# Retention with both directions stacked on 128 partitions, and another order of the attention steps, in a two-block transformer kernel

## The chip, the cores and the metric

The kernel runs on one core of one Trainium2 chip. The metric is the device time of one execution in microseconds (us); smaller is better. The engines are called as the profile calls them: PE (TensorE, the matrix engine), DVE (VectorE), ACT (ScalarE), POOL (GpSimd) and SP (the queue that issues most transfers). Each runs its own program in order; they meet at semaphores.

## What is computed

Two transformer blocks on one sequence of 512 tokens with 1024 features, all in float32. The first block (feed-forward, gated linear attention with convolution, feed-forward) is not touched. In the second, one projection feeds a neighbourhood attention (8 heads, 4 column blocks) and a bidirectional retention (4 heads, 4 chunks of 128 tokens). The part that the change rewrites, cut from the reference:

```python
def retention_scan(q, k, v, log_gamma, include_diag):
    ...
    s = jnp.einsum('bnihd,bnjhd->bnhij', qc, kc) * dmat
    intra = jnp.einsum('bnhij,bnjhe->bnihe', s, vc)
    zeta = jnp.exp(log_gamma[:, None] * (c - 1 - idx)[None, :])
    chunk_kv = jnp.einsum('bnjhd,hj,bnjhe->nbhde', kc, zeta, vc)
    ...
    _, prev = lax.scan(step, jnp.zeros((bsz, heads, dk, dv), F32), chunk_kv)
    xi = jnp.exp(log_gamma[:, None] * (idx + 1.0)[None, :])
    cross = jnp.einsum('bnihd,nbhde,hi->bnihe', qc, prev, xi)
    return (intra + cross).reshape(bsz, seq, heads, dv)

def bidirectional_retention(q, k, v, lg_fwd, lg_bwd):
    flip = lambda t: jnp.flip(t, axis=1)
    fwd = retention_scan(q, k, v, lg_fwd, True)
    bwd = flip(retention_scan(flip(q), flip(k), flip(v), lg_bwd, False))
    return fwd + bwd
```

A head has 64 query and key features and 128 value features. The sum over both directions is normalised per head (`head_group_norm`), gated by a SiLU and stands beside the attention's output before the product with `w_out_2`.

## The kernel before

**Units.** The whole program is a list of units. A unit is the product of one weight block of 1024 x 128 with the activations: 8 slices of 128 rows, each with three products of 128x512 (high part by high, low by high, high by low: lines 1294 to 1296), so 24 products. Unit u needs its weights split: a transfer brings them to `raw`, ACT copies them to `wh` (`hi`, line 360), DVE subtracts to get `wl` (`lo`, line 714). Three buffers go round, so at unit u ACT and DVE prepare unit u+2, and ACT may only do so once unit u-1 is done.

**The stage.** The change lies in the 16 units from `U0["rot"]`: I call them steps 0 to 15. Steps 0 to 3 make the rotary queries and keys (`RQ`, `RK`), steps 4 to 11 the attention's queries and keys (`NQ`, `NK`), steps 12 to 15 the gates. Retention and attention are cut into pieces that are written between the units by hand, in one loop `for n in range(16)` in each engine's program. On PE a piece stands in the middle of the unit (`ret_mid`, after 12 of its 24 products) or behind it. Nothing but this written order decides what runs when.

**Attention.** A piece p (0 to 15) is a pair of heads hp = p // 4 and a column block p % 4. Pieces go in pairs: `na_s(p)` on PE makes the scores of p and p+1 (line 1582, banks 3 and 4); DVE adds the bias and takes the maxima (`na_s`, lines 1127 and 1129), ACT takes the exponentials (`na_e`, line 611), DVE divides by the sums (`na_x`, lines 1136 to 1139), PE transposes (`na_t(p)`, line 1594, bank 5 for even p and 3 for odd p), ACT copies the transposed scores out (`na_t`, line 616), PE multiplies with the values (`na_o(p)`, line 1606, bank 6). POOL prepares the bias tiles (line 341).

**Retention.** Two heads share the 128 partitions of `RQ` and `RK`. PE transposes the keys of a pair (`ret_k`, line 1516), ACT scales them into `KF` and `KB` (line 590), PE makes the chunk states forward and backward (`ret_kv`, line 1529, 64 columns of a head at a time), DVE runs the recurrences (lines 1096 and 1099) into `SF` and `SB` and scales the queries (`ret_q`, lines 1106 and 1108) into `QF` and `QB`. Per head: `ret_s(h)` makes the scores (line 1540), DVE applies the decay (line 1113), `ret_o(h)` makes the output in bank 2 from 10 products (line 1552 within the chunk, lines 1554 and 1556 across chunks, these on the head's 64 partitions), ACT copies and squares it (lines 602 and 603), `ret_n(h)` sums the squares over the partitions in bank 7 (line 1324), DVE makes the mean (line 730), ACT the inverse root (`rows`, lines 370 to 374), DVE corrects it and scales the output (`ret_y`, lines 734, 736 and 1119). Before the change step n of the loop has, behind the unit on PE, `na_t(p)`, `na_t(p + 1)`, `na_o(p)`, `na_o(p + 1)` with p = 2(n - 7), and `na_s(p + 2)`.

Of the kernel before, what the change touches and what calls it, by code (L numbers as in the profile page):

```python
# [1852 lines left out]
```

## Time and profile before

| what | us |
|---|---|
| median of 3 runs | 1859.44 (1859.05 to 1859.75) |
| the profiled execution, its own time | 1860.06 |
| span from its first to its last instruction | 1858.3 |
| PE busy | 1833.1 |
| DVE busy | 968.1 |
| ACT busy | 618.3 |

The rows in the section further down are of these kinds. The page sums busy time by engine and follows back the chain of work that ended last. A row of the timeline has the start in us from the span's start, how long the merged instructions took, engine, line, operation, tiles written and read, shapes and count; in brackets the engine's idle time ahead of it and what ended it. Products overlap in the pipeline, so the distance between two starts says what a product costs, and not its own duration. A float32 product of the small pieces shows as two records. A row of the windows view gives for one stretch the busy time of each engine with the number of its instructions, and behind them the granted clock of PE as a share of full speed (1.00 is 2.4 GHz, 0.50 is 1.2 GHz).

### The profile page before, as it was taken

What the parts mean: (1) busy time and instruction counts of PE and PEld (TensorE: products, weight loads), DVE (VectorE), ACT (ScalarE), POOL (GpSimd) and SP (SyncE); (2) the same over time, 40 slices, a digit from 0 to 9 for tenths busy, and PEclk for the clock granted to TensorE, in tenths of its full rate; (3) what the DMA queues carried; (4) which work ended last, traced back from release to release, by engine and by line L of the source; (5) the groups of instructions that cost most, each with busy time, mean ns of one, the idle gap of its engine ahead of it and who ended that gap; (6) DMA issues with size and microseconds to landing.
All of it is one profiled execution on the core that took longest, in us unless ns stands there. A gap on an engine that the chain in (4) does not pass through costs nothing.

```text
span 1858.3 us, 20334 instructions
## 1 busy us (share of the span) xinstructions
PE 1833.1 (99%) x8370; PEld 1507.5 (81%) x8370; DVE 968.1 (52%) x1275; ACT 618.3 (33%) x881; POOL 33.5 (2%) x34
## 2 busy tenths in 40 slices
PE   8999999999999999999999999999999999999998
PEld 6888888878888888888888888888776788888887
DVE  6444434637765534455543443465567664535354
ACT  6222313344332223323422222244445432222133
POOL 0000000000000000000000000000221000000000
PEclk9999999999999999999999999999999999999999
DMA  5332332332122232323233233233411233232322
GB/s 172 93 101 94 99 102 85 97 103 80 57 91 95 98 102 91 102 91 102 91 102 96 98 92 101 87 98 128 131 41 46 82 100 102 92 102 91 102 91 69
DMA packets 52812, 176.38 MB, mean 95 GB/s; under 512 B 6336, under 2 KB 9024, under 8 KB 52720
## 3 DMA queue, kind: packets, MB, share of 16 engines
q1 hardware_dynamic: 51520, 172.51, 29.0%
q8 instruction: 67, 1.10, 0.2%
q0 software_dynamic: 448, 1.24, 0.2%
q10 hardware_dynamic: 752, 1.33, 0.2%
q14 instruction: 25, 0.20, 0.0%
HBM read 170.86 MB, written 2.10 MB: 93 GB/s over the span
## 4 chain that ended last, share of the span: by engine, by line
PE 94%; DVE 3%; ACT 2%; issue 1%; DMA 0%; SPq 0%; DVEq 0%
PE ps L1294 28%; PE ps L1295 28%; PE ps L1296 28%; PE ps L1314 2%; PE ps L1316 1%; PE ps L1315 1%; DVE wl L714 1%; PE ps L1324 0%; PE ps L1450 0%; PE ps L1582 0%; PE ps L1552 0%; DVE tm L1127 0%; PE ps L1453 0%; PE ps L1438 0%; DVE X L800 0%
## 5 line engine op out<-in xcount | busy, mean ns | idle before, releaser
L1294 PE MATMUL ps<-Hhi,wh 128*128 128x512 f32 x1544 | 610.9, 396 | 6.8 <-DVE Hlo L719 6.8
L1295 PE MATMUL ps<-Hlo,wh 128*128 128x512 f32 x1544 | 603.0, 391 | 0.0
L1296 PE MATMUL ps<-Hhi,wl 128*128 128x512 f32 x1544 | 602.9, 390 | 0.0
L714 DVE TENSOR_TENSOR wl<-raw,wh 128x1024 fp32r<-128x1024 f32 (+1 forms) x320 | 388.0, 1213 | 127.1 <-ACT wh L360 125.0
L360 ACT ACTIVATE wh<-raw 128x1024 fp32r<-128x1024 f32 (+1 forms) x320 | 332.3, 1039 | 321.3 <-PE ps L1296 301.4
L1294 PEld LDWEIGHTS ps<-Hhi,wh 128*128 128x128 f32 x1544 | 291.0, 188 | 73.8 <-issue 11.1
L1295 PEld LDWEIGHTS ps<-Hlo,wh 128*128 128x128 f32 x1544 | 291.2, 189 | 61.9 <-issue 2.6
L1296 PEld LDWEIGHTS ps<-Hhi,wl 128*128 128x128 f32 x1544 | 291.0, 188 | 61.2
L1294 PE MATMUL ps<-Ahi,wh 128*128 128x512 f32 x792 | 308.2, 389 | 0.3 <-DVE Alo L1155 0.3
L1296 PE MATMUL ps<-Ahi,wl 128*128 128x512 f32 x792 | 308.1, 389 | 0.0
L1295 PE MATMUL ps<-Alo,wh 128*128 128x512 f32 x792 | 308.1, 389 | 0.0
L762 DVE TENSOR_TENSOR tm<-ps,R 128x512 f32<-128x512 f32 x128 | 88.5, 691 | 197.5 <-PE ps L1296 197.4
L1294 PEld LDWEIGHTS ps<-Ahi,wh 128*128 128x128 f32 x792 | 148.7, 188 | 31.5 <-DVE Alo L1155 0.7
L1296 PEld LDWEIGHTS ps<-Ahi,wl 128*128 128x128 f32 x792 | 148.7, 188 | 30.9
L1295 PEld LDWEIGHTS ps<-Alo,wh 128*128 128x128 f32 x792 | 148.7, 188 | 30.8
L770 DVE TENSOR_TENSOR Alo<-tm,Ahi 128x512 fp32r<-128x512 f32 x92 | 63.7, 692 | 70.5 <-ACT Ahi L402 34.2
L800 DVE SCALAR_TENSOR_TENSOR X<-ps,X 128x512 f32<-128x512 f32 x48 | 33.1, 690 | 96.7 <-PE ps L1296 96.7
L766 DVE TENSOR_TENSOR X<-ps,X 128x512 f32<-128x512 f32 x47 | 32.5, 691 | 95.5 <-PE ps L1296 95.5
L402 ACT ACTIVATE Ahi<-tm 128x512 fp32r<-128x512 f32 x44 | 27.8, 633 | 163.2 <-DVE tm L792 163.2
L387 ACT ACTIVATE tm<-tm 128x512 f32<-128x512 f32 x44 | 27.8, 632 | 163.1 <-DVE tm L762 163.1
L792 DVE TENSOR_TENSOR tm<-ps,tm 128x512 f32<-128x512 f32 x44 | 30.4, 691 | 77.1 <-PE ps L1296 77.0
L676 ACT ACTIVATE Ahi<-tm 128x512 fp32r<-128x512 f32 x32 | 20.2, 633 | 124.1 <-DVE tm L1224 124.1
(256 smaller groups left out, 1192.2 us busy)
## 6 DMA issues: line engine op xcount, KB each, us to landing
raw<-in_w_gu SPq DMA_DIRECT2D x87, 512.0 KB, 3.3
raw<-in_w_d SPq DMA_DIRECT2D x32, 512.0 KB, 3.5
raw<-in_w_up SPq DMA_DIRECT2D x32, 512.0 KB, 3.3
raw<-in_w_dn SPq DMA_DIRECT2D x32, 512.0 KB, 3.6
raw<-in_w_d SPq DMA_DIRECT2D x16, 384.0 KB, 3.1
raw<-in_w_v SPq DMA_DIRECT2D x8, 512.0 KB, 3.6
raw<-in_w_cc SPq DMA_DIRECT2D x8, 512.0 KB, 3.3
raw<-in_w_cu SPq DMA_DIRECT2D x8, 512.0 KB, 3.4
```

Source lines behind the costliest of these rows:

```text
L360: act.activation(WH[u % 3][:, 0:n], RAW[u % 3][:, 0:n], ACT.Copy).then_inc(s["wh"], 1)
L387: act.activation(TA[2 + j % 2], TA[j % 2], ACT.Silu).then_inc(s["silu"], 1)
L714: dve.tensor_tensor(WL[u % 3][:, 0:n], RAW[u % 3][:, 0:n], f32(WH[u % 3][:, 0:n]), ALU.subtract).then_inc(s["wl"], 1)
L762: dve.tensor_tensor(dst, BK[BANK[u]][:, :], R[:, :], ALU.mult).then_inc(s["ev"], 1)
L766: dve.tensor_tensor(X[:, n, :], BK[BANK[u]][:, :], X[:, n, :], ALU.add).then_inc(s["ev"], 1)
L770: dve.tensor_tensor(Alo[:, j, :], src, f32(Ahi[:, j, :]), ALU.subtract).then_inc(s["al"], 1)
L792: dve.tensor_tensor(TA[6 + j % 2], BK[BANK[u + 1]][:, :], TA[4 + j % 2], ALU.mult).then_inc(s["ev"], 1)
L800: dve.scalar_tensor_tensor(out=X[:, n, :], in0=BK[BANK[u]][:, :], scalar=0.5, in1=X[:, n, :], op0=ALU.mult, op1=ALU.add).then_inc(s["ev"], 1)
L1294: pe.matmul(ps, wh[:, c], hi[:, k, :], start=(k == 0), stop=False)
L1295: pe.matmul(ps, wh[:, c], lo[:, k, :], start=False, stop=False)
L1296: last = pe.matmul(ps, wl[:, c], hi[:, k, :], start=False, stop=(k == nb - 1))
L1314: pe.matmul(ps, Hhi[:, k, tc], wh[:, c], start=(k == 0), stop=False)
```

## The change

**Both directions on one set of partitions.** For each head, forward keys stand in columns 0 to 63 and backward keys in columns 64 to 127 of `KFB`; a product `ret_kv(h)` gives both states of a chunk in 128 partitions, four per head. The states lie in `SFB[h]` (forward in partitions 0 to 63, backward in 64 to 127, zeros where a direction has no earlier chunk) and the scaled queries likewise in `QFB[h]`, each with a buffer of its own per head. `ret_o(h)` is then 8 products over all 128 partitions instead of 10. ACT copies the first state of each direction (`ret_kv` on ACT), DVE sets zeros and does the rest. The scores of two heads are made together (`ret_s(hp)`), in two banks (`RB_S`). Outputs and states take banks from `RB_O` and `RB_KV`, and `ret_n(h)` writes its sums over the bank of the output that has been copied out.

**Another order.** The pieces of retention stand at other places (listed below the diff). On PE the outputs of the attention come one step later, between the two transposes, which both use bank 5: `na_t(p)`, `na_o(p - 2)`, `na_o(p - 1)`, `na_t(p + 1)`, `na_s(p + 2)` in every step; a third buffer (`PT`) holds the copies. On DVE `lo(u + 2)` now stands ahead of `na_x(p)`, and `ret_kv`, `ret_mean` and `ret_y` behind it. On ACT `rows` and `ret_o` stand ahead of the copies of the transposed scores in steps 9 to 11 (`rows` alone in 11). `na_s(12)` and `na_s(14)` move from the middle of units 12 and 13 to behind units 12 and 13. The transfers of `VB` are issued three units earlier on SP.

```diff
@@ tiles
-    RT_S, RT_Q, RT_G, RT_O = [1, 0, 2, 1], [2, 1, 0, 2], [0, 1, 0, 2], [2, 1, 0, 1]
+    RT_S, RT_Q, RT_G = [1, 0, 0, 2], [2, 1, 1, 0], [2, 1, 0, 2]
+    RB_S, RB_O, RB_KV = [5, 4, 2, 6], [2, 7, 2, 7], [2, 6, 5, 6]
+    PT = [TA[4], TA[5], PT2[:, :]]
@@ ACT
+        def ret_kv(h):
+            kv = four(BK[RB_KV[h]][:, :])
+            act.wait_ge(s["rkv"], h + 1)
+            act.activation(SFB[h][0:64, 1, :], kv[0:64, 0, :], ACT.Copy).then_inc(s["rkc"], 1)
+            act.activation(SFB[h][64:P, 2, :], kv[64:P, 3, :], ACT.Copy).then_inc(s["rkc"], 1)
...
-            act.activation(TA[4 + p % 2], BK[3 if p % 2 else 5][:, :], ACT.Copy).then_inc(s["ntc"], 1)
+            act.activation(PT[p % 3], BK[5][:, :], ACT.Copy).then_inc(s["ntc"], 1)
...
+            if n == 6:
+                ret_o(0)
+                ret_o(1)
+                ret_kv(2)
+                ret_kv(3)
+            if n in (7, 9, 10, 11):
+                rows(7 + (7, 9, 10, 11).index(n), TA[6], TA[7], TA[8])
+            if n in (9, 10):
+                ret_o(n - 7)
             if 7 <= n < 15:
                 na_t(p)
+                if n in (9, 11, 13):
+                    na_o((n - 9) // 2)
                 na_t(p + 1)
...
-            if 6 <= n < 12:
+            if 6 <= n < 14:
                 na_e(p + 2)
...
-            if n in (6, 7, 9, 10):
-                rows(7 + (6, 7, 9, 10).index(n), TA[6], TA[7], TA[8])
@@ DVE
+        def ret_kv(h):
+            kv = four(BK[RB_KV[h]][:, :])
+            own.add(dve.memset(SFB[h][0:64, 0, :], 0.0))
+            own.add(dve.memset(SFB[h][64:P, 3, :], 0.0))
+            dve.wait_ge(s["rkc"], 2 * h + 2)
+            for step in range(2):
+                own.add(dve.scalar_tensor_tensor(out=SFB[h][0:64, 2 + step, :], in0=SFB[h][0:64, 1 + step, :],
...
+            lo(u + 2)
             if 7 <= n < 15:
                 na_x(p)
-            lo(u + 2)
...
+            if n == 5:
+                ret_kv(0)
+                ret_kv(1)
+                ret_s(0)
+                ret_s(1)
+                ret_q(2)
...
+            if n == 7:
+                ret_kv(2)
+                ret_kv(3)
+                ret_mean(0)
+            if n == 8:
+                ret_s(2)
                 ret_s(3)
...
+            if 9 <= n < 13:
+                ret_y(n - 9)
+                if n < 12:
+                    ret_mean(n - 8)
@@ PE
+        def ret_o(h):
+            b = RB_O[h]
+            pe.wait_ge(s["rst"], h + 1)
+            pe.wait_ge(s["rq"], h + 1)
+            pe.wait_ge(s["rsd"], h + 1)
...
+                pe.matmul(BK[b][:, tc], RV[:, c, h * P:h * P + P], RT[RT_S[h]][:, tc], start=True, stop=False)
+                p = pe.matmul(BK[b][:, tc], SFB[h][:, c, :], QFB[h][:, tc], start=False, stop=True)
...
         def na_t(p):
-            b = 3 if p % 2 else 5
             pe.wait_ge(s["nxd"], p + 1)
-            if p >= 2:
-                pe.wait_ge(s["ntc"], p - 1)
...
+            if p == 0:
+                pe.wait_ge(s["rst"], 3)
+            else:
+                pe.wait_ge(s["ntc"], p)
...
             if n == 4:
-                ret_k(0)
+                ret_s(0)
             if n == 5:
-                ret_s(0)
+                ret_o(0)
             if n == 6:
-                na_s(0)
-                ret_n(0)
+                ret_kv(1)
             if 7 <= n < 15:
                 na_t(p)
+                if n == 7:
+                    ret_s(1)
+                else:
+                    na_o(p - 2)
+                    na_o(p - 1)
                 na_t(p + 1)
...
+            if 6 <= n < 14:
                 na_s(p + 2)
```

In the middle of the units PE now has `ret_k(0)` in step 3, `ret_kv(0)` (heads 0 and 1) in 4, `ret_k(1)` in 5, `ret_o(1)` and `ret_n(0)` in 6, `ret_n(1)` in 7, `ret_o(2)` in 9, `ret_n(2)` and `ret_o(3)` in 10, `ret_n(3)` in 11 and `na_o(14)`, `na_o(15)` in 15.

**Where it shows: ACT in step 9.** Line 360 (362 after the change) is the copy `hi` of the weights, 602 and 603 (611 and 612) copy and square a retention output, 616 (625) copies transposed scores, 611 (620) is an exponential, 370 to 374 (372 to 376) are `rows`. Before:

```order
L360 ACTIVATE wh1_58<-raw1_55 128x1024 [waits s_pe,s_raw1]
L602 ACTIVATE YH_123<-ps 128x512 [waits s_ro]
L603 ACTIVATE SS_64<-ps 128x512
L616 ACTIVATE tm4_70<-ps 128x512 [waits s_nat]
L616 ACTIVATE tm5_71<-ps 128x512 [waits s_nat]
L611 ACTIVATE tm2_68,small_82<-tm2_68,small_82 128x256 [waits s_nmx]
```

and after:

```order
L362 ACTIVATE wh1_58<-raw1_55 128x1024 [waits s_pe,s_raw1]
L372 ACTIVATE tm7_73<-tm6_72 128x512 [waits s_nm]
L374 ACTIVATE tm7_73<-tm7_73 128x512 [waits s_ao]
L376 ACTIVATE tm8_74<-tm7_73 128x512 [waits s_ao]
L611 ACTIVATE YH_127<-ps 128x512 [waits s_ro]
L612 ACTIVATE SS2_65<-ps 128x512
L625 ACTIVATE tm5_71<-ps 128x512 [waits s_nat]
L629 ACTIVATE Ahi_52<-ps 128x512 [waits s_nop]
L625 ACTIVATE PT2_124<-ps 128x512 [waits s_nat]
```

The three instructions of `rows`, the first of which waits for DVE's mean (`nm`), have moved from behind the step's exponentials to ahead of its first copy of transposed scores.

**DVE in step 9.** Line 714 (731) is `lo`; 1136 to 1139 (1165 to 1168) are `na_x`; 734, 736 and 1119 (751, 753 and 1148) are `ret_y`; 1113 is a decay of scores, 730 (1143) the mean. Before:

```order
L1136 RECIPROCAL small_82<-small_82 128x2 [waits s_nex]
L1138 TENSOR_SCALAR tm1_67<-tm1_67,small_82 128x256 [waits s_vo]
L1139 TENSOR_SCALAR tm1_67<-tm1_67,small_82 128x256
L714 TENSOR_TENSOR wl1_61<-raw1_55,wh1_58 128x1024 [waits s_wh]
L1113 TENSOR_TENSOR SS2_65<-ps,DG_113 128x512 [waits s_rsc]
L1187 SCALAR_TENSOR_TENSOR NK_102<-ps,R_63 128x512 [waits s_pe]
```

and after:

```order
L731 TENSOR_TENSOR wl1_61<-raw1_55,wh1_58 128x1024 [waits s_wh]
L1165 RECIPROCAL small_82<-small_82 128x2 [waits s_nex]
L1167 TENSOR_SCALAR tm0_66<-tm0_66,small_82 128x256 [waits s_vo]
L1168 TENSOR_SCALAR tm0_66<-tm0_66,small_82 128x256
L1165 RECIPROCAL small_82<-small_82 128x2 [waits s_nex]
L1167 TENSOR_SCALAR tm1_67<-tm1_67,small_82 128x256 [waits s_vo]
L1168 TENSOR_SCALAR tm1_67<-tm1_67,small_82 128x256
L751 SCALAR_TENSOR_TENSOR tm6_72<-tm8_74,tm6_72 128x512 [waits s_na]
L753 SCALAR_TENSOR_TENSOR tm6_72<-tm6_72,tm7_73 128x512 [waits s_vo]
L1148 TENSOR_TENSOR YH_127<-YH_127,tm6_72 128x512 [waits s_vo]
L1143 TENSOR_SCALAR tm6_72<-ps 128x512 [waits s_vo,s_nsum]
```

The weights' `lo` now stands ahead of `na_x`, and the mean for which ACT's `rows` waits is the last of the eleven.

**PE behind unit 9.** Line 1594 (1620) transposes, 1606 (1634) is the attention's output, 1582 (1609) its scores. Before:

```order
L1594 MATMUL ps<-ident_77,tm0_66 128x128 [waits s_ntc,s_nxd]
L1594 MATMUL ps<-ident_77,tm0_66 128x128 x3
L1594 MATMUL ps<-ident_77,tm1_67 128x128 [waits s_ntc,s_nxd]
L1594 MATMUL ps<-ident_77,tm1_67 128x128 x3
L1606 MATMUL ps<-tm4_70,VB_103 64x128 [waits s_nal,s_ntc]
```

and after:

```order
L1620 MATMUL ps<-ident_77,tm0_66 128x128 [waits s_ntc,s_nxd]
L1620 MATMUL ps<-ident_77,tm0_66 128x128 x3
L1634 MATMUL ps<-PT2_124,VB_103 64x128 [waits s_vb2,s_ntc]
L1634 MATMUL ps<-PT2_124,VB_103 64x128 x3
L1634 MATMUL ps<-tm4_70,VB_103 64x128 [waits s_vb3,s_ntc]
L1634 MATMUL ps<-tm4_70,VB_103 64x128 x3
L1620 MATMUL ps<-ident_77,tm1_67 128x128 [waits s_ntc,s_nxd]
L1620 MATMUL ps<-ident_77,tm1_67 128x128 x3
L1609 MATMUL ps<-NK_102,NQ_101 128x256 [waits s_nsd,s_ev]
```

The outputs of the step before stand between the two transposes, and the second transposes wait for the copy of the first (`ntc`).

## Rows read from the trace of the kernel before

**Rows 1.** The page: busy time of PE; the chain that ended last, by engine.
```profile
PE 1833.1 (99%) x8370; PEld 1507.5 (81%) x8370; DVE 968.1 (52%) x1275; ACT 618.3 (33%) x881; POOL 33.5 (2%) x34
...
PE 94%; DVE 3%; ACT 2%; issue 1%; DMA 0%; SPq 0%; DVEq 0%
```

**Rows 2.** Windows (us): busy by engine, PEclk, DMA; the stage, and a stretch behind a wait.
```profile
1300.10:1453.05 152.95, 143.91 (x817) 111.59 (x816) 98.20 (x168) 75.85 (x165) 29.96 (x24) 0.99 0.23 70
...
1338.90:1342.40 3.50, 3.50 (x10) 2.68 (x10) 1.43 (x2) 0.00 (x0) 0.00 (x0) 0.51 0.41 118
```

**Rows 3.** Timeline of PE: units, retention's pieces, two waits.
```profile
1300.10 0.39 PE L1294 MATMUL ps<-Hhi,wh 128*128 128x512 f32 x1
...
1327.08 0.39 PE L1296 MATMUL ps<-Hhi,wl 128*128 128x512 f32 x1
...
1330.61 0.88 PE L1529 MATMUL ps<-RV,KF 128*64 128x128 f32 x12
...
1332.07 0.50 PE L1294 MATMUL ps<-Hhi,wh 128*128 128x512 f32 x1
...
1337.32 1.16 PE L1540 MATMUL ps<-RQ,RK 64*128 64x128 f32 x8 [2.19 <-DVE QB L1108]
...
1342.85 0.39 PE L1552 MATMUL ps<-SS,RV 128*128 128x128 f32 x2
...
1347.20 0.53 PE L1294 MATMUL ps<-Hhi,wh 128*128 128x512 f32 x1
...
1351.28 1.12 PE L1324 MATMUL ps<-RS,ones 128*128 128x512 f32 x2
...
1355.00 0.38 PE L1552 MATMUL ps<-SS,RV 128*128 128x128 f32 x2
...
1358.67 0.50 PE L1294 MATMUL ps<-Hhi,wh 128*128 128x512 f32 x1
...
1427.38 0.63 PE L1594 MATMUL ps<-ident,tm 128*128 128x128 f32 x4 [1.50 <-DVE tm L1127]
```

**Rows 4.** Timeline of PE in the first block: 28 small records on all 128 rows.
```profile
475.56 0.60 PE L1450 MATMUL ps<-ST,VT 128*128 128x128 f32 x4
...
478.69 0.49 PE L1419 MATMUL ps<-ident,KS 128*128 128x128 f32 x3
```

**Rows 5.** Timeline of PE behind unit 10: transposes, scores, outputs, sum of squares.
```profile
1403.57 1.04 PE L1594 MATMUL ps<-ident,tm 128*128 128x128 f32 x8
1405.43 1.14 PE L1582 MATMUL ps<-NK,NQ 64*128 64x256 f32 x8 [0.83 <-ACT tm L616]
1406.50 1.15 PE L1606 MATMUL ps<-tm,VB 128*64 128x128 f32 x16
1407.58 1.13 PE L1324 MATMUL ps<-RS,ones 128*128 128x512 f32 x2
```

**Rows 6.** Timeline of DVE around steps 6 and 7, and one recurrence.
```profile
1332.87 0.73 DVE L1099 SCALAR_TENSOR_TENSOR SF<-SF,small,ps 128x128 f32<-128x128 f32 x2
...
1351.41 0.69 DVE L1127 TENSOR_TENSOR tm<-ps,tm 128x512 f32<-128x512 f32 x1 [0.40 <-PE ps L1582]
...
1354.05 0.68 DVE L730 TENSOR_SCALAR tm<-ps 128x512 f32<-128x512 f32 x1
1354.65 0.16 DVE L1136 RECIPROCAL small<-small 128x2 f32<-128x2 f32 x1
...
1355.11 0.35 DVE L1139 TENSOR_SCALAR tm<-tm,small 128x256 f32<-128x256 f32 x1
...
1358.09 1.22 DVE L714 TENSOR_TENSOR wl<-raw,wh 128x1024 fp32r<-128x1024 f32 x1 [1.90 <-ACT wh L360]
1359.23 0.69 DVE L734 SCALAR_TENSOR_TENSOR tm<-tm,tm 128x512 f32<-128x512 f32 x1
...
1360.68 0.69 DVE L1119 TENSOR_TENSOR YH<-YH,tm 128x512 f32<-128x512 f32 x1
```

**Rows 7.** Timeline of ACT: steps 6 and 7, and the start of the gates.
```profile
1355.17 0.61 ACT L370 ACTIVATE tm<-tm 128x512 f32<-128x512 f32 x1
...
1357.02 1.04 ACT L360 ACTIVATE wh<-raw 128x1024 fp32r<-128x1024 f32 x1
1358.78 0.60 ACT L602 ACTIVATE YH<-ps 128x512 f32<-128x512 f32 x1 [0.72 <-PE ps L1554]
...
1439.87 1.28 ACT L625 ACT_TABLE_LOAD   x1
...
1443.15 1.04 ACT L360 ACTIVATE wh<-raw 128x1024 fp32r<-128x1024 f32 x1
```

More of the change, by code:

```diff
@@ L566, in act_program @@
         act.wait_ge(s["lgv"], 2)
-        own.add(act.activation(E128, LG[:, 8:12], ACT.Exp, scale=128.0))
+        own.add(act.activation(E128, LG[:, 12:16], ACT.Exp, scale=128.0))
         act.wait_ge(s["dgm"], 1)
@@ new lines, in ret_q @@
+        def ret_q(h):
+            hs = slice(64 * (h % 2), 64 * (h % 2) + 64)
+            dve.wait_ge(s["rot"], 1 + h // 2 * 2)
+            dve.wait_ge(s["rxf"], h // 2 * 2 + 2)
+            own.add(dve.tensor_tensor(four(QFB[h][0:64, :]), four(RQ[hs, h // 2, :]),
+                                      XF[hs, :].unsqueeze(1).broadcast_to([64, 4, P]), ALU.mult))
+            dve.tensor_tensor(four(QFB[h][64:P, :]), four(RQ[hs, h // 2, :]),
+                              XB[hs, :].unsqueeze(1).broadcast_to([64, 4, P]), ALU.mult).then_inc(s["rq"], 1)
@@ L1116, in ret_y, with ret_mean @@
+        def ret_s(h):
+            dve.wait_ge(s["rsc"], h // 2 + 1)
+            dve.tensor_tensor(four(RT[RT_S[h]]), four(BK[RB_S[h]][:, :]),
+                              DG[:, h, :].unsqueeze(1).broadcast_to([P, 4, P]), ALU.mult).then_inc(s["rsd"], 1)
+        def ret_mean(h):
+            dve.wait_ge(s["nsum"], 7 + h)
+            own.wait()
+            dve.tensor_scalar(TA[6], BK[RB_O[h]][:, :], 1.0 / P, EPS, ALU.mult, ALU.add).then_inc(s["nm"], 1)
         def ret_y(h):
@@ L1533, in ret_s @@
-        def ret_s(h):
-            hs = slice(64 * (h % 2), 64 * (h % 2) + 64)
-            if h % 2 == 0:
-                pe.wait_ge(s["rq"], h // 2 + 1)
-            else:
-                pe.wait_ge(s["rsd"], h)
+                pe.wait_ge(s["rsd"], 1)
+                pe.wait_ge(s["rst"], 2)
+            for h in (2 * hp, 2 * hp + 1):
+                for c in range(4):
+                    p = pe.matmul(BK[RB_KV[h]][:, c * P:c * P + P], KFB[:, h % 2, c, :], RV[:, c, h * P:h * P + P],
+                                  start=True, stop=True)
+                p.then_inc(s["rkv"], 1)
@@ L1539, in ret_s @@
+        def ret_s(hp):
+            pe.wait_ge(s["rot"], 2 * hp + 2)
+            if hp == 1:
+                pe.wait_ge(s["nm"], 7)
+                pe.wait_ge(s["rst"], 4)
             for c in range(4):
[L1540 to L1541 removed]
+                for j in range(2):
+                    hs, b = slice(64 * j, 64 * j + 64), RB_S[2 * hp + j]
+                    p = pe.matmul(BK[b][:, c * P:c * P + P], RK[hs, hp, c * P:c * P + P], RQ[hs, hp, c * P:c * P + P],
+                                  start=True, stop=True)
```

224 lines of the change are left out of this document (89 added, 135 removed).

## The prediction, made before the changed kernel was run

> **What bounds the kernel now.** I read the page first: PE is busy 99% of the span and makes up 94% of the chain that ended last [rows 1]. So a change pays what it takes from PE or makes PE wait, and nothing else. The windows view then bounds the stage: steps 0 to 15 last 152.95 us [rows 2]. All that the change moves lies there (the earlier `VB` transfers reach back a little, onto a queue that runs three units ahead). In the timeline, 120 products of five units run from 1300.10 to the start of the last at 1327.08 [rows 3]: 26.98 / 119 = 0.227 us each, 5.44 us a unit, 87.0 us for 16 units. The other 66 us are small pieces, waits, and one stretch at half the clock. The longest wait is 2.19 us, for DVE's `QB` [rows 3]; behind it PE ran at a granted clock of 0.51 for 3.5 us [rows 2], in which 10 records stand where 3.5 / 0.227 = 15 would elsewhere. At 1.2 GHz for 3.5 us half of it is lost: 1.8 us.
>
> **The small pieces, priced.** On all 128 rows of the array, 28 float32 records take 478.69 - 475.56 = 3.13 us, 0.112 each [rows 4].
> - `ret_o`, before: 1355.00 to the next unit product at 1358.67 is 3.67 us a head [rows 3]. After: 8 products, 16 records, all on 128 rows as in rows 4: 16 x 0.112 = 1.79. Four heads: -7.5 us.
> - `ret_kv`, before: 1330.61 to 1332.07 is 1.46 us a pair [rows 3], 24 records at 0.061, two halves of 64 columns side by side. After: 16 records on the whole array, 1.79. Two pairs: +0.7. Here a rule speaks against the change. The Trainium skill (TensorEngine Tiling (Array Packing), Theoretical Speedup) gives up to twice the speed for products at most 64 wide on a tiled array. The trace agrees (0.061 against 0.112); stacking gives this up, and by the rule or by the rows the loss is the same small one.
> - Retention's scores, before: about 1.1 us where they stand alone (8 records, 1.16 with their tail) and 0.7 at the end of `ret_o` (1342.85 to 1347.20 is 4.35, less 3.67) [rows 3], some 3.4 for four heads. After, two heads on two row groups. Attention's scores are built like that: 8 records of 256 columns in 1406.50 - 1405.43 = 1.07 us [rows 5], 0.13 each, though 256 columns one after the other would need 0.22. So a pair costs between 1.1 (overlapped) and 1.8 (not); I take 1.1: -1.2.
> - Unchanged in work: four transposes 0.45, attention scores 1.07, a pair of outputs 1.08 (1406.50 to 1407.58), a sum of squares 0.9 of the 1.13 it shows [rows 5]. One more change of array shape per step (transposes, outputs, transposes, scores): 0 to 0.2 each, within the rounding of the steps below.
>
> If nothing ever waited, the steps would add up to 129 us, 131 with the shape changes: 22 us below the stage of before. So the question is who is late.
>
> **The chain behind the scores.** In steps 7 to 14 PE needs the normalised scores of the pair that it made at the end of the step before. I call the end of those scores E; it is the start of the next unit. From rows, with E of step 6 at 1351.28, where the sum of squares takes over on PE [rows 3] (DVE starts at 1351.41 [rows 6]):
> - bias, maxima, exponentials: ACT's next work starts at 1355.17 [rows 7], E + 3.9.
> - `hi`, next in ACT's order: 1.04 [rows 7]. `lo` follows 1.07 behind `hi`'s start (1357.02, 1358.09): starts at E + 4.95. The next DVE work starts 1.14 later (1359.23) [rows 6]: E + 6.1.
> - the first half of `na_x`: 1354.65 to 1355.11 + 0.35 = 0.81 [rows 6]: E + 6.9; both halves 1.54: E + 7.65.
>
> Before, `na_x` stood ahead of `lo`: its first half was done at 1355.46, E + 4.2, sooner than the unit. Now PE is ready for the transposes at E + 5.45 in a step with nothing in mid unit, and waits 1.5 us. The order rows of DVE leave no other way.
>
> In steps 9 to 11 it goes on. DVE does `ret_y`, 1359.23 to 1360.68 + 0.69 = 2.14 [rows 6], then the mean (0.68, as at 1354.05): E + 10.45. ACT's `rows` wait for that mean: 1355.17 to 1357.02 = 1.85: E + 12.35. In steps 9 and 10 ACT then copies and squares a retention output, about 0.5 apiece since 0.60 overlaps the next [rows 7]: E + 13.3. Only then comes the copy of the first transposed scores, of the same form and so 0.6: E + 13.9. PE's second transposes need that copy, since both write bank 5. They start at E + 14.0 in steps 9 and 10, at E + 13.0 in 11. Queued behind them on PE are the next scores, and behind these the next unit and the next chain: nothing can run ahead.
>
> **The steps after, one by one (us).** 0 to 2: 16.3. 3: unit, four transposes, and 0.3 of waiting for the rotated keys (DVE ends `turn(1)` about when mid unit comes; 0 to 0.3): 6.2. 4: unit + 1.79 + 1.1 = 8.3. 5: unit + 0.45 + 1.79, and a wait of 1.0 (DVE: `turn(3)`, `lo`, two recurrences, a decay; a recurrence is 2 x 0.65 by the 0.73 of a pair of steps [rows 6], plus 0.25 for the zeros, ahead of which POOL's bias tiles may slow `lo`; 0.7 to 1.3): 8.7. 6: unit + 1.79 + 0.9 + 1.79 + 1.07 = 11.0. 7: `na_t(0)` waits for `ret_kv(2)` as well, since bank 5 held those states: 7.65 + 1.55 = E + 9.2 instead of 6.35; retention's scores wait for the other recurrence and the mean, E + 11.4; then 1.1 + 0.45 + 1.07: 14.1. 8: transposes at 7.0, outputs wait for two decays on DVE (7.65 + 1.3 = 8.95), then 1.08 + 0.45 + 1.07: 11.6. 9 and 10: 14.0 + 0.45 + 1.07 = 15.6 each. 11: 14.6. 12 and 13: 7.0 + 0.45 + 1.08 + 0.45 + 1.07 = 10.2 each (with the shape changes). 14: ACT has taken up the gate's table load and first gate ahead of `hi`. From the load at 1439.87 to `hi` at 1443.15 is 3.3 [rows 7], so `hi` ends at 3.9 + 3.3 + 1.04 = 8.3, `lo` at 9.5, the first half of `na_x` at E + 10.3; then 0.45 + 1.08 + 0.45: 12.4. 15: unit + 1.1 + 0.2 = 6.7. Behind it nothing is late that was not before.
>
> Sum: 161.5, against 152.95: **+8.5 us**. It contains 32 us of PE waiting, where before PE was idle for 152.95 - 143.91 = 9 [rows 2] and the slow clock cost 1.8.
>
> **The clock.** The trace has one fall to 1.2 GHz in the stage, behind a wait of 2.19 us; behind the wait of 1.50 at 1427.38 [rows 3] it stayed at 2.4. The new waits of steps 7 (3 and 1.7), 9 (5), 10 (4), 11 (4.5) and 14 (4.8) are all as long or longer, so I expect a fall at each, worth up to 1.8 by the row. Where a unit runs slowly and the next step waits anyway, the loss is absorbed; only the transposes and scores ahead of the next E count, about 1 us each in steps 7 to 11, and all 1.8 in 14: +6, with 0 and +10 as ends. The Trainium skill (TensorE: Matmul & The Clock Gate, What's actually happening) says that the gate's resting state is the slow one and that activity releases it; by that rule each long wait costs, which agrees with the one fall seen. It gives no other sum.
>
> **Forecast.** +8.5 + 6 = +14.5 us on the profiled execution's own 1860.06 (its span 1858.3 and 1.8 around it): 1874.6. That execution is 0.6 above the median, so the median comes to **1874.0**.
>
> **Rivals.**
> - *The clock does not fall, or only where it is absorbed.* For it: only one fall in 153 us so far. Time 1859.4 + 8.5 = 1868. Chance 0.15.
> - *The clock stays low over steps 7 to 11.* Against it: the fall seen lasted 3.5 us with PE busy. It decides once the small pieces between waits are too little activity to bring it back: each step's tail of 2.7 us then takes up to twice as long and units of 10 us exceed the first transposes' time by 3: +24 in all, 1883. Chance 0.08.
> - *Faster.* DVE and ACT keep up after all and the change keeps its shorter PE work: mechanism and place would be `ret_y` and the mean of steps 9 to 11 done while DVE waits for `wh` rather than behind it. In-order engines forbid this by the order rows; it would need E + 14.0 to shrink below PE's own 8.9 to 9.8. Up to -22: 1838. From a shortening of the chains of steps 9 to 11 by 3 us each on, the sign turns if the clock also holds. Chance 0.08.
> - *Chains shorter than priced by 1 to 2 us each,* as when DVE overlaps more than rows show: 1862 to 1867, of which half lies within 0.2%. Chance 0.07.
>
> The forecast's own case has the remaining 0.62, between 1868 and 1880. The range 1863 to 1883 leaves out the faster rival and a bit on each side, under 2 in 10. About 0.2% (3.7 us) is what a measurement of this kernel can tell from no change. Slower by more: 0.62 + 0.15 + 0.08 + 0.03 = 0.88; within: 0.04; faster: 0.08.
>
> **What would show it.** Right: a wait of some 5 us ahead of the second transposes of step 9, put down to ACT's copy, 4 or more in 10 and 11; about 1.5 us ahead of the first transposes of steps 12 and 13, put down to `na_x`; 2.8 us ahead of `na_t(0)` with the recurrence as releaser; some 4.8 in step 14. Outputs of retention 1.8 us a head. Several stretches at a granted clock of 0.5. Wrong: second transposes of step 9 before E + 10, steps 9 and 10 shorter than 12 us each, or PE's small records of `ret_o` farther apart than 0.112.

## The result, and the profile after

The changed kernel takes **1880.1 us** in the median (1879.1 to 1880.9, four runs), the kernel before 1859.45 (1859.05 to 1859.75) beside it. The ratio is 1.011, with a 95% interval of 1.009 to 1.013: the change makes the kernel about 20 us slower. The forecast was 1874.0 with a range of 1863 to 1883. The profiled execution of after took 1880.53 us, 0.4 above its median, so its trace can be read as it stands.

The page of after, against [rows 1]: PE busy, the chain that ended last by engine, and the granted clock in 40 slices.

```profile
PE 1835.7 (98%) x8338; PEld 1510.0 (80%) x8338; DVE 970.2 (52%) x1291; ACT 621.5 (33%) x889; POOL 31.8 (2%) x34
...
PEclk9999999999999999999999999999988999999999
...
PE 92%; DVE 4%; ACT 2%; issue 1%; DMA 0%; SPq 0%; DVEq 0%
```

PE has 32 matmul records fewer than before (8338 against 8370) and is busy 2.6 us *longer*; two slices of the clock are down. The windows view of after says where: the stage (steps 0 to 15), and two stretches in which the clock was down. Columns as in [rows 2]: length, busy time by engine, granted clock, DMA.

```profile
1300.02:1473.31 173.29, 146.27 (x785) 114.12 (x784) 100.25 (x184) 79.12 (x173) 28.29 (x24) 0.90 0.20 63
...
1361.95:1372.19 10.24, 7.75 (x34) 5.86 (x35) 4.87 (x9) 4.17 (x9) 2.51 (x2) 0.50 0.01 2
...
1392.67:1399.50 6.83, 4.22 (x15) 2.90 (x16) 1.74 (x3) 3.51 (x7) 2.51 (x2) 0.50 0.01 2
```

The stage went from 152.95 us [rows 2] to 173.29, +20.3, which is the whole difference of the spans (1878.5 - 1858.3 = 20.2). PE is not busy for 173.29 - 146.27 = 27.0 us of it, where it was 9.0 before. And the clock of TensorE is at half (1.2 GHz) in five stretches of 10.2, 6.8, 3.4, 6.8 and 6.8 us, 34 us in all, where before there was one of 3.4.

Who is waited for, by the waits view of PE in the stage of after (total us, times, longest):

```profile
PE ps L1620 <- ACT tm L625: 9.2, 3, 5.0
PE ps L1620 <- DVE tm L1168: 5.8, 2, 4.6
PE ps L1620 <- ACT PT L625: 4.2, 1, 4.2
PE ps L1620 <- DVE SFB L1117: 3.0, 1, 3.0
PE ps L1574 <- DVE tm L1143: 2.1, 1, 2.1
PE ps L1634 <- DVE RS L1137: 1.4, 1, 1.4
PE ps L1589 <- DVE SS L1137: 1.3, 1, 1.3
```

L1620 are the transposes of the attention weights, L625 ACT's copy of transposed weights out of PSUM, L1168 the normalisation `na_x`. Before, the transposes waited twice for DVE, 1.5 us [rows 3] and 0.5, and never for ACT's copy.

The longest wait, in step 9, is followed here through the timelines of DVE, ACT and PE, put together in order of time. The step starts at E = 1381.20, with the unit behind the scores.

```profile
1386.15 1.22 DVE L731 TENSOR_TENSOR wl<-raw,wh 128x1024 fp32r<-128x1024 f32 x1 [2.11 <-ACT wh L362]
1387.30 0.16 DVE L1165 RECIPROCAL small<-small 128x2 f32<-128x2 f32 x1
...
1388.75 0.69 DVE L751 SCALAR_TENSOR_TENSOR tm<-tm,tm 128x512 f32<-128x512 f32 x1
...
1390.99 0.69 DVE L1143 TENSOR_SCALAR tm<-ps 128x512 f32<-128x512 f32 x1
...
1391.72 0.63 ACT L372 ACTIVATE tm<-tm 128x512 f32<-128x512 f32 x1 [5.60 <-DVE tm L1143]
...
1393.58 0.58 ACT L611 ACTIVATE YH<-ps 128x512 f32<-128x512 f32 x1
...
1394.53 0.60 ACT L625 ACTIVATE tm<-ps 128x512 f32<-128x512 f32 x1
...
1395.28 1.09 PE L1620 MATMUL ps<-ident,tm 128*128 128x128 f32 x4 [5.02 <-ACT tm L625]
1396.29 2.08 PE L1609 MATMUL ps<-NK,NQ 64*128 64x256 f32 x8
```

Read it downwards: DVE computes `lo` (L731) for 1.2 us while the softmax's sums lie ready, only then `na_x` (L1165 to L1168), then `ret_y` (L751 on) and the group mean (L1143) at E + 9.8. ACT, idle for 5.60 us, waits for that mean, does three row operations and retention's copy and square, and at E + 13.3 the copy of the first transposed weights. PE has waited 5.02 us. The last row has a second lesson: the eight score records take 2.08 us, where the eight of the kernel before take 1.14 at full clock in [rows 5]. They lie in the stretch 1392.67 to 1399.50 of the windows above, with the granted clock at 0.50.

### The profile page after: what moved, and what is told of

Same layout as the page of the kernel before. It is cut to its first block, busy times and chain, and to the rows that moved or that the text cites. A ratio compares the mean times of both kernels' runs of the same rounds, so it can differ in the third digit from the quotient of the medians.

```text
span 1878.5 us, 20299 instructions
## 1 busy us (share of the span) xinstructions
PE 1835.7 (98%) x8338; PEld 1510.0 (80%) x8338; DVE 970.2 (52%) x1291; ACT 621.5 (33%) x889; POOL 31.8 (2%) x34
## 4 chain that ended last, share of the span: by engine, by line
PE 92%; DVE 4%; ACT 2%; issue 1%; DMA 0%; SPq 0%; DVEq 0%
PE ps L1328 28%; PE ps L1330 28%; PE ps L1329 28%; PE ps L1348 2%; PE ps L1349 1%; PE ps L1350 1%; DVE wl L731 1%; PE ps L1609 1%; DVE tm L1156 1%; PE ps L1620 0%; ACT wh L362 0%; PE ps L1484 0%; PE ps L1634 0%; PE ps L1358 0%; PE ps L1487 0%
## 5 line engine op out<-in xcount | busy, mean ns | idle before, releaser
L731 DVE TENSOR_TENSOR wl<-raw,wh 128x1024 fp32r<-128x1024 f32 (+1 forms) x320 | 387.7, 1212 | 133.3 <-ACT wh L362 131.5
L1328 PEld LDWEIGHTS ps<-Hhi,wh 128*128 128x128 f32 x1544 | 292.1, 189 | 74.8 <-issue 12.1
L1329 PEld LDWEIGHTS ps<-Alo,wh 128*128 128x128 f32 x792 | 148.7, 188 | 30.8
L1330 PEld LDWEIGHTS ps<-Ahi,wl 128*128 128x128 f32 x792 | 148.7, 188 | 30.8
L693 ACT ACTIVATE Ahi<-tm 128x512 fp32r<-128x512 f32 x32 | 20.2, 633 | 124.1 <-DVE tm L1258 124.1
```

Of the source, the lines that this page charges most:

```text
L731: dve.tensor_tensor(WL[u % 3][:, 0:n], RAW[u % 3][:, 0:n], f32(WH[u % 3][:, 0:n]), ALU.subtract).then_inc(s["wl"], 1)
L1328: pe.matmul(ps, wh[:, c], hi[:, k, :], start=(k == 0), stop=False)
L1329: pe.matmul(ps, wh[:, c], lo[:, k, :], start=False, stop=False)
L1330: last = pe.matmul(ps, wl[:, c], hi[:, k, :], start=False, stop=(k == nb - 1))
```

## Experiments

Eight kernels were run, in two batches, each batch with its own runs of the kernel before (1859.5 and 1860.3 us). Stage lengths and PE's busy time are from each one's profiled execution, which can lie a little off its median: x1's is 1.6 us below, x2's 1.1 above.

### x1 and x2: each order undone alone; x3: both

x1 puts the normalisation back ahead of `lo` on DVE. x2 puts ACT's row operations for retention behind the copies of the transposed weights.

x1, on DVE:

```diff
-            lo(u + 2)
             if 7 <= n < 15:
                 na_x(p)
+            lo(u + 2)
```

x2, on ACT:

```diff
-            if n in (7, 9, 10, 11):
-                rows(7 + (7, 9, 10, 11).index(n), TA[6], TA[7], TA[8])
             if n in (9, 10):
                 ret_o(n - 7)
             if 7 <= n < 15:
                 na_t(p)
                 if n in (9, 11, 13):
                     na_o((n - 9) // 2)
                 na_t(p + 1)
+            if n in (7, 9, 10, 11):
+                rows(7 + (7, 9, 10, 11).index(n), TA[6], TA[7], TA[8])
```

> The changed kernel with one edit on DVE: na_x(p) ahead of lo(u + 2) again, as in the kernel before. Theory (the chains behind the scores set the steps, and waits bring the clock down): the first transposes of steps 12 and 13 no longer wait, each step 1.3 us shorter; steps 7, 8, 9, 10, 11 and 14 each 1.4 to 1.6 shorter, because their chains lose 1.1 us of lo and 0.4 of waiting for the weights; 12 us in all, and 3 us less at the slow clock: about 1865. The wait ahead of the second transposes of step 9 falls from 5.0 to 3.5. Rival (the excess is the slow clock alone, set off by PE's many small pieces): at most the 1.5 us of each wait, no fall of the clock gone, steps 9 to 11 as long as before: 1875 or more.

> The changed kernel with one edit on ACT: rows in steps 7, 9, 10 and 11 behind the copies of both transposed scores (ahead of na_e), not ahead of them. Theory: the waits of 5.0, 3.6 and 4.2 us ahead of the second transposes of steps 9 to 11 vanish, the steps go from 17.1, 16.5 and 16.1 to 10.4, 11.3 and 10.2, and the falls of the clock there with them: 19 us, about 1861. Waits of steps 7, 8, 12, 13 and 14 stay. Rival (the copies are late for another reason, DVE being behind): rows then delay na_e and hi by 1.85 us, the next step's transposes wait instead, and the gain is under 8 us: 1872 or more.

> Both edits at once (na_x ahead of lo on DVE, rows behind the copies on ACT). Theory: they remove different waits, so the gains add: steps 9 to 11 at 10.3, 11.2 and 9.5, 12 and 13 at 8.9; left are some 3 us in step 7 (the recurrences), 1.4 in 8, 3.3 in 14. 22 us of waits and 9 of the slow clock gone: about 1849, which is 0.6% faster than the kernel before. Rival (the stacked retention itself costs PE time): no faster than the kernel before, 1860 or more.

Measured: x1 **1866.2** us (ratio to before 1.0035, 1.0022 to 1.0048), x2 **1866.4** (1.0033, 1.0021 to 1.0046), x3 **1853.0** (0.9965, 0.9952 to 0.9978). Each order accounts for some 14 us, both for 27 of the 1880: the effects add up. With both, the changed kernel is faster than the kernel before, by 0.35%. The windows view of their stages (x1, x2, x3):

```profile
1299.97:1457.50 157.53, 138.79 (x786) 109.43 (x785) 100.73 (x184) 79.15 (x173) 28.15 (x24) 0.96 0.21 67
```
```profile
1301.01:1460.32 159.31, 141.71 (x785) 111.06 (x784) 99.78 (x184) 79.70 (x173) 28.36 (x24) 0.94 0.21 68
```
```profile
1299.82:1445.02 145.20, 136.08 (x785) 107.93 (x784) 100.50 (x184) 79.38 (x173) 28.72 (x24) 0.98 0.22 73
```

PE executes the same matmuls in all of them, yet its busy time falls from 146.27 (after) to 141.71, 138.79 and 136.08 as the clock rises from 0.90 to 0.94, 0.96 and 0.98. So part of what an order costs is not waiting but slow matmuls behind the wait. By their times the rivals (1875 or more, 1872 or more, 1860 or more) are out.

x1 came within 1.2 us of its expectation; x2 missed by 5 us and x3 by 4. The expectation of x2 let the waits of the other steps stay as they were. Its steps 9 to 11 are as short as expected (32.6 us together against 31.9), but steps 8 and 12 grew from 11.7 to 13.2 and from 10.2 to 13.0: PE waits there 1.2 and 2.4 us for the normalised weights, where in after it did not. That is what the rival of x2 said of the next step's transposes, though it takes less of the gain than the rival had it. All such waits of x2, in five steps:

```profile
PE ps L1620 <- DVE tm L1168: 10.0, 5, 4.6
```

x1 shows that a wait need not bring the clock down. It still waits 3.6 us in step 9, yet the granted clock is 1.00 from the start of that wait until the next is nearly over:

```profile
1387.27:1405.00 17.73, 11.50 (x74) 9.05 (x74) 9.93 (x19) 10.92 (x23) 2.53 (x2) 1.00 0.10 30
```

In step 14 it waits 3.17 us without a fall, and x3 waits the same 3.17 us at the same place and falls behind it, for 3.4 us.

### xfill: the waits filled with work

To see what the clock alone costs, 24 products of 128x512 were put where PE waits in after (their output is overwritten, nothing reads it). Everything else is unchanged.

```diff
+        def fill(n, at):
+            k = {5: (1, 0), 7: (3, 2), 8: (1, 1), 9: (0, 4), 10: (0, 3), 11: (0, 3), 12: (1, 0), 13: (1, 0), 14: (4, 0)}.get(n, (0, 0))[at]
...
+            for _ in range(k):
+                pe.wait_ge(s["ev"], EVN[PREV[u]])
+                pe.matmul(BK[BANK[u]][:, :], ones[:, :], f32(Hhi[:, 0, :]), start=True, stop=True)
```

> The changed kernel with 24 idle products added on PE (ones by a slice of the activations, 128x512, float32, 1.07 us each), whose results the next unit overwrites: 1 in step 5, 5 in 7, 2 in 8, 4 in 9, 3 each in 10 and 11, 1 each in 12 and 13, 4 in 14, each where PE waits. They are extra work, nothing is left out. Theory (the waits are set by DVE and ACT, and the excess of the stage over 161.5 us is the slow clock): the added 26 us lie in the waits, PE never rests for long, the clock stays at its full level and the kernel gets faster by some 10 us: 1869 to 1871. Rival (the clock has little to do with it, the steps were priced too short): the stage keeps its 173 us or grows by the overhang: 1880 or more; and if the waits were not real idle time, up to 1906.

Measured: **1873.0** us (ratio 1.0073, 1.0058 to 1.0088), 2 us above the range expected. With 24 useless products more, the kernel is 7.1 us *faster* than after. The window of the stage of xfill, and from its PE timeline the filling of step 7 and the scores at that step's end:

```profile
1300.15:1465.69 165.54, 155.13 (x833) 114.03 (x832) 100.19 (x184) 79.17 (x173) 28.42 (x24) 1.00 0.20 64
```
```profile
1358.11 2.74 PE L1666 MATMUL ps<-Hhi,ones 128*128 128x512 f32 x6
...
1366.64 0.63 PE L1620 MATMUL ps<-ident,tm 128*128 128x128 f32 x4 [1.49 <-ACT tm L625]
1367.20 1.14 PE L1609 MATMUL ps<-NK,NQ 64*128 64x256 f32 x8
```

The granted clock is 1.00 over the whole stage, and the scores take 1.14 us. xfill's stage is 173.29 - 165.54 = 7.75 us shorter, all of it in steps 7, 9, 10, 11, 14 and 15, behind the long waits.

### xctl: the same products elsewhere

```diff
-            k = {5: (1, 0), 7: (3, 2), 8: (1, 1), 9: (0, 4), 10: (0, 3), 11: (0, 3), 12: (1, 0), 13: (1, 0), 14: (4, 0)}.get(n, (0, 0))[at]
+            k = {0: (6, 0), 1: (6, 0), 2: (6, 0), 3: (6, 0)}.get(n, (0, 0))[at]
```

> The changed kernel with the same 24 products of 128x512 that filled PE's waits in the earlier run (each 0.95 us there: 2.84 us for three), put six behind each of steps 0 to 3 instead, where PE does not wait. It tells apart whether the earlier gain came from where they stood. Theory, that the gain was the clock kept up in the waits: 24 x 0.93 = 22 us more and the falls of the clock of the changed kernel stay where they were (34 us at half): 1880 + 22 = about 1902 us. Rival, that something else of the edit made the program faster (its code, its waits on banks, a longer busy history of PE ahead of the stage): well under 1890 us, or no falls of the clock in steps 7 to 14.

Measured: **1901.0** us (ratio 1.0217, 1.0202 to 1.0232), 21 more than after. The stage of xctl:

```profile
1300.29:1494.04 193.75, 165.60 (x833) 122.07 (x832) 100.22 (x184) 79.16 (x173) 28.27 (x24) 0.92 0.17 55
```

The trace has its five falls again (10.2, 3.4, 3.4, 6.8, 6.8 us). The products are worth 7 us where PE would idle; in steps 0 to 3, where it would not, they cost about 0.84 us each (20 us in all). This pair shows that the falls of the stage depend on PE's idling there, and that keeping PE busy in the waits keeps the clock up.

### b1: the cheap-looking order in the kernel before

```diff
-            if 7 <= n < 15:
-                na_x(p)
             lo(u + 2)
+            if 7 <= n < 15:
+                na_x(p)
```


> The kernel before with one order of the changed kernel: on VectorE the weights' low part is computed ahead of the normalisation of the attention weights in steps 7 to 14 (1.2 us of work in front of it). Theory: in the kernel before the next product on PE that needs the normalised weights comes behind other attention work, so that 1.2 us later is mostly hidden: 1859.5 + 0 to 3 = about 1861 us, where the same order in the changed kernel cost 1880.1 - 1866.2 = 13.9 us. Rival, that the order costs alike wherever it stands (8 steps x 1.2 us and the clock): 1869 us or more.

Measured: **1868.9** us (ratio 1.0046, 1.0031 to 1.0061), so +8.5. The theory's 0 to 3 is out. The time is the rival's (1869 or more), but not for its reason, that 8 times 1.2 us would be waited. Below stand the window of the stage of b1, two of PE's waits in it, the same two in before, and the row of b1's first wait:

```profile
1299.05:1461.19 162.14, 150.81 (x817) 116.14 (x816) 97.21 (x168) 76.18 (x165) 29.95 (x24) 0.95 0.21 66
```
```profile
PE ps L1540 <- DVE QB L1108: 4.5, 2, 2.3
PE ps L1594 <- DVE tm L1139: 3.3, 2, 2.0
```
```profile
PE ps L1540 <- DVE QB L1108: 3.2, 2, 2.2
PE ps L1594 <- DVE tm L1139: 0.5, 1, 0.5
```
```profile
1336.28 2.07 PE L1540 MATMUL ps<-RQ,RK 64*128 64x128 f32 x8 [2.21 <-DVE QB L1108]
```

Against [rows 2] the stage grew by 162.14 - 152.95 = 9.2. PE idles 11.33 us instead of 9.04: the waits grew by only 2.3, within what the theory allowed. But PE's busy time for the same 817 records grew by 150.81 - 143.91 = **6.9 us**, and the trace has four stretches at half clock (6.8, 3.4, 3.4, 3.4 us, 17.1 in all) instead of one of 3.4; half of the 13.7 us added is 6.8.

Not all of that is the edit's. 1.4 of the 9.2 us lie in steps 5 and 6, where the edit changes nothing. PE's wait for `QB` is 2.21 us there against 2.19 before [rows 3], but the fall of the clock began while PE still waited and lasted 6.8 us, where before it began 1.6 us behind the wait and lasted 3.4; the scores next to the wait took 2.07 us instead of 1.16. The other steps grew by 7.8 us: 2.3 of waiting and 5.5 of busy time for the same matmuls, with 10.2 us more at half clock. Some two thirds of the price of this edit is the clock, by one execution of each kernel.

### x3g and best: the waits that x3 still had

In x3, the waits view of PE in the stage shows:

```profile
PE ps L1620 <- DVE tm L1168: 3.2, 1, 3.2
PE ps L1574 <- DVE tm L1143: 2.1, 1, 2.1
PE ps L1620 <- DVE SFB L1117: 1.6, 1, 1.6
PE ps L1589 <- DVE SS L1137: 1.3, 1, 1.3
PE ps L1634 <- DVE RS L1137: 0.9, 1, 0.9
```

x3g moves the gates' first products out of step 14, where ACT's table load stood ahead of `hi`. best does that too and reorders DVE in steps 5 to 8.

Both, on ACT (and alike on DVE, where `rg_out(1)` of step 15 stands behind `lo`):

```diff
             if n == 15:
+                rg_silu(1)
+                rg_out(1)
                 na_o(3)
-            if n > 12:
-                rg_silu(n - 13)
-                rg_out(n - 13)
+            if n > 13:
+                rg_silu(2 * n - 28)
+                rg_out(2 * n - 28)
```

best alone, on DVE:

```diff
+            if n == 5:
+                ret_kv(0)
+                ret_kv(1)
+                ret_s(0)
+                ret_s(1)
+            if n == 7:
+                ret_kv(3)
+            if n == 8:
+                ret_s(2)
+                ret_s(3)
             if 7 <= n < 15:
                 na_x(p)
             lo(u + 2)
...
             if n == 5:
-                ret_kv(0)
-                ret_kv(1)
-                ret_s(0)
-                ret_s(1)
                 ret_q(2)
             if n == 6:
                 ret_q(3)
-            if n == 7:
-                ret_kv(2)
-                ret_kv(3)
-                ret_mean(0)
-            if n == 8:
-                ret_s(2)
-                ret_s(3)
...
+            if n == 6:
+                ret_mean(0)
+                ret_kv(2)
             if 6 <= n < 14:
                 na_s(p + 2)
```

> The kernel with both orders and of the three further moves only the gates' (the gates' products with G one step later on ScalarE and VectorE). Theory: the wait of 3.2 us in step 14 ends with the weights of head pair 3 (normalised behind the gate's two operations on VectorE) and goes to under 0.5, and the fall of the clock at 1435.3 us (3.4 us, 1.7 lost) goes with it: 1853.0 - 2.9 - 1.7 = about 1848.5 us. Rival, that step 15 or the output projection behind it then waits for the gate's products: 1851 to 1853 us, with a new wait in step 15 or behind.

> Both orders of the earlier run (the normalisation of the weights ahead of the second half of the H difference on VectorE, the row copies behind the transposes' copies on ScalarE), and three more moves: step 5's state and score work on VectorE ahead of the weights' low part; the group mean and one state copy moved from step 7 to step 6, the pair of the last scores to the start of step 8; the gates' products with G moved one step later on ScalarE and VectorE. Theory: what is left in the kernel with both orders are waits on PE of 1.3 us in step 5, 1.6 and 2.1 in step 7, 0.9 in step 8 and 3.2 in step 14 (9.1 us by its waits' rows) and 6.8 us in which the clock is at half (3.4 us lost). Taking away most of the waits and with them the two falls: 145.2 - 9 - 3.4 = 132.8 us for the sixteen steps, 1853.0 - 12.4 = about 1841 us. Rival, that the waits only move by a step because PE and VectorE are both near their sum in steps 7 and 14: the time stays at 1849 to 1853 us.

Measured: x3g **1850.8** us (ratio 0.9948, 0.9933 to 0.9963), best **1843.35** (1842.1 to 1844.0; ratio 0.991, 0.989 to 0.993), each some 2 us above what was expected. best is 17 us faster than the kernel before and 37 faster than the changed kernel. The stages of x3g and of best:

```profile
1299.91:1443.04 143.13, 134.40 (x786) 106.46 (x784) 100.57 (x185) 79.24 (x173) 28.72 (x24) 0.99 0.24 76
```
```profile
1300.03:1435.19 135.16, 132.62 (x786) 105.62 (x784) 100.18 (x185) 79.24 (x173) 27.93 (x24) 1.00 0.25 80
```

x3g's step 14 went from 12.1 to 7.6 us and its fall of the clock there is gone, but step 15 grew from 7.2 to 9.3: its rival holds for half. In best all that is left of PE's waits in the stage is

```profile
PE ps L1334 <- DVE Alo L1174: 2.3, 1, 2.3
PE ps L1595 <- DVE SS L1139: 0.2, 1, 0.2
```

and the clock stays at 1.00. Step 9 of best, whose E is 1368.95, to be laid beside step 9 of after:

```profile
1373.91 1.23 DVE L733 TENSOR_TENSOR wl<-raw,wh 128x1024 fp32r<-128x1024 f32 x1
1375.06 0.68 DVE L753 SCALAR_TENSOR_TENSOR tm<-tm,tm 128x512 f32<-128x512 f32 x1
...
1376.35 0.60 PE L1626 MATMUL ps<-ident,tm 128*128 128x128 f32 x4
...
1376.99 0.60 ACT L625 ACTIVATE tm<-ps 128x512 f32<-128x512 f32 x1 [2.11 <-PE ps L1626]
...
1379.09 0.62 ACT L372 ACTIVATE tm<-tm 128x512 f32<-128x512 f32 x1
```

The copy that PE needs (L625) now runs at E + 8.0, as soon as PE's transposes are there, and the row operation (L372) after it at E + 10.1, where nobody waits for it in this step. The same instructions, in another order, and the step is 10.6 us instead of 17.1.

### All of them side by side

| kernel | time | stage | PE busy | PE idle | at half clock |
|---|---|---|---|---|---|
| before | 1859.45 | 152.95 | 143.91 | 9.0 | 3.4 |
| b1 | 1868.85 | 162.14 | 150.81 | 11.3 | 17.1 |
| after | 1880.1 | 173.29 | 146.27 | 27.0 | 34.1 |
| x1 | 1866.2 | 157.53 | 138.79 | 18.7 | 13.7 |
| x2 | 1866.4 | 159.31 | 141.71 | 17.6 | 20.5 |
| x3 | 1853.0 | 145.20 | 136.08 | 9.1 | 6.8 |
| x3g | 1850.8 | 143.13 | 134.40 | 8.7 | 3.4 |
| best | 1843.35 | 135.16 | 132.62 | 2.5 | 0 |

PE idle is the stage less PE busy; the last column adds the stretches that the trace gives at 0.5. From best upwards PE's busy time follows that column: 132.62 plus half of it gives 134.3, 136.0, 142.9 and 139.5 for x3g, x3, x2 and x1, against 134.40, 136.08, 141.71 and 138.79. It is an upper bound where part of the slow time is itself idle, as in after, which gives 149.7 against 146.27.

What the change takes from PE is read from before and best: before's 143.91 less half of its 3.4 us is 142.2, best's is 132.6. **PE is busy for 9.6 us less at full clock.** The restacking accounts for some 8 of it by the rows: 7.6 for four `ret_o` (3.67 to 1.78 each) and 1.2 for the scores, less 0.8 for the states. The other 1.6 are not traced to a piece; before and best differ in the order of the pieces too, and no run has one without the other. In after, all of it and more is lost to the order around it.

## Why the prediction was right, and what was mis-sized

The prediction held in its direction and in its mechanism: PE waits behind chains that DVE's and ACT's new orders lengthen, and the waits bring the clock down. It was 6.1 us short of the median, and its errors of any size lie on the same side, so the time did not come out by terms that cancel.

**PE's pieces.** Right. From the PE timeline of after: `ret_o` of one head lasts from 1343.15 to 1344.93, 1.78 us where 1.79 was priced; the state products from 1348.55 to 1350.43, 1.88 where 1.79 was.

```profile
1343.15 0.38 PE L1589 MATMUL ps<-SS,RV 128*128 128x128 f32 x2
...
1344.93 1.02 PE L1595 MATMUL ps<-RS,ones 128*128 128x512 f32 x2
1348.55 1.95 PE L1562 MATMUL ps<-RV,KFB 128*128 128x128 f32 x16
1350.43 0.92 PE L1609 MATMUL ps<-NK,NQ 64*128 64x256 f32 x6
```

A pair of retention's scores, between a unit at each side, takes 1.10 us (1329.88 to 1330.98 in step 4), the overlapped end of the bracket. The sum "if nothing ever waited", 129 to 131, can be laid beside PE's busy time in best, 132.6, 1.6 more than its upper figure.

**The chain behind the scores.** Right in every link in step 9: the mean came at E + 9.8 (priced 9.8 to its start), ACT's rows ended and the copy began at E + 13.3 (priced 13.3), the second transposes at E + 14.1 (priced 14.0). The waits of steps 9, 10 and 11 were 5.0, 3.7 and 4.2 us (priced 5, 4, 4.5), of step 13 1.2 and of 14 4.6 (priced 1.5 and 4.8). The wait of 1.5 us priced in step 12 is not there: its unit ran for 2.8 us at half clock and came no sooner than the weights, and the step lasts 10.2 us in after as in xfill. x1 and x2 each take one link out and gain 14 us.

**The steps.** Predicted without the clock, and measured in after and in xfill, where the clock stays up:

| step | predicted | xfill | after |
|---|---|---|---|
| 0 to 4 | 30.8 | 31.0 | 31.0 |
| 5 | 8.7 | 9.3 | 9.3 |
| 6 | 11.0 | 11.2 | 11.2 |
| 7 | 14.1 | 16.6 | 18.1 |
| 8 | 11.6 | 11.7 | 11.7 |
| 9 | 15.6 | 15.7 | 17.1 |
| 10 | 15.6 | 15.7 | 16.5 |
| 11 | 14.6 | 14.7 | 16.1 |
| 12, 13 | 20.4 | 20.5 | 20.5 |
| 14 | 12.4 | 12.4 | 14.1 |
| 15 | 6.7 | 6.8 | 7.9 |
| sum | 161.5 | 165.5 | 173.3 |

The 11.8 us between the sum of 161.5 and the stage measured have three parts.
- **Step 7, +2.5.** A term was left out. ACT's row operations stand ahead of the copy of the transposed weights in step 7 as in 9 to 11, and there too they wait for DVE's mean. The prediction followed PE's retention scores behind that mean and left ACT out. From DVE's, ACT's and PE's timelines of after:

```profile
1363.07 0.69 DVE L1143 TENSOR_SCALAR tm<-ps 128x512 f32<-128x512 f32 x1
...
1363.79 0.63 ACT L372 ACTIVATE tm<-tm 128x512 f32<-128x512 f32 x1 [7.38 <-DVE tm L1143]
...
1365.77 0.60 ACT L625 ACTIVATE tm<-ps 128x512 f32<-128x512 f32 x1
...
1366.51 1.09 PE L1620 MATMUL ps<-ident,tm 128*128 128x128 f32 x4 [0.57 <-ACT tm L625]
```

  The copy comes at 1365.77, E + 14.3, and the second transposes at E + 15.0, whatever the clock does: they are at 1366.64 in xfill as well, also E + 15.0.
- **Step 5, +0.6** (its wait was 1.35 us, estimated 1.0, from 0.7 to 1.3), and 0.9 over all other steps, a tenth here and there.
- **The clock, +7.75**, estimated 6 with 0 to 10 as ends. In after the falls were at the waits named, though x1 has waits of 3.6 and 3.17 us without one. But a fall was taken to last 3.5 us, as in the one before; they lasted 3.4, 6.8 or 10.2. Half of 34.1 us would be 17 us, of which 7.75 shows in the time. The rest was absorbed, as the prediction had it: a unit that runs slowly between two waits only shortens the second.

In all the forecast was 6 us short; 3.1 of it is in steps 5 and 7, 1.75 in the clock.

**The rivals.** "The clock does not fall" gave 1868 and is refuted by the five falls. "Stays low over steps 7 to 11" gave 1883: it came back in each step, though late. "Faster" needed DVE and ACT to keep up, which the orders as written forbid; with the orders changed it came true. That the rival had put 1838 and best measured 1843.35 does not bear it out: it spoke of the orders as written, and best is another kernel. "Chains shorter than priced by 1 to 2 us" gave 1862 to 1867 and is refuted: steps 9 to 11 last 15.7, 15.7 and 14.7 us in xfill, without the clock, against 15.6, 15.6 and 14.6.

**Not settled.** Whether the 9.6 us of PE's work could be had with before's distribution of the pieces over the steps was not tried, nor what would remove best's last wait of 2.3 us. What decides whether the clock falls at a wait, and for how long, is open: the same wait in the same code gave a fall of 3.4 us in one execution and 6.8 in another, and 3.17 us in step 14 gave one in x3 and none in x1. Each trace is one execution, so the column at half clock would differ somewhat in another. In xfill the filling may itself delay a step by a tenth or two; 7.75 would then be a lower bound of what the clock costs in after.

## What to carry to other kernels

When a change shortens the work of the engine that bounds the kernel, the in-order queues of the engines that feed it need to be ordered anew: put what that engine waits for first (here the normalisation ahead of `lo`, the PSUM copy ahead of the row operations), and work that nobody in this step waits for behind it. Price a wait of some us on TensorE twice, once as idle time and once as the matmuls that run slowly behind it; in b1 2.3 us of added waits went with 7.8 us in the steps that the edit touches. For each engine walk the whole queue of *every* step: ACT's queue in step 7, not walked here, held the largest omission.

## What the runs showed of the hardware

- TensorE's granted clock fell to half in or behind waits of 2 to 5 us among small pieces, and stayed there for 3.4, 6.8 or 10.2 us (after, b1, x1, x2, x3), mostly longer than the one fall in the kernel before suggested. PE was not idle meanwhile: in the stretch of 10.2 us of after it was busy for 7.75. The length of the wait alone does not decide: waits of 3.6 and 3.17 us in x1 and of 2.3 in best had no fall, nor had one of 1.5 before [rows 3], while one of 2.19 us had.
- Work that nobody needs can pay: 24 products put into the waits made the kernel 7.1 us faster, and the same 24 put where PE was busy anyway made it 21 us slower. The granted clock is 0.90 over the stage of after and 1.00 over that of xfill. The Trainium skill (TensorE: Matmul & The Clock Gate, What's actually happening) ties the granted clock to the activity of the array; the traces of these two agree.
- The gains of two reorderings added up (14 + 14 against 27 us), though x2 alone moved 3.7 us of waiting into steps 8 and 12, which x3 does not have.
